# One decoder layer on one core: zeros written in one later transfer, first products and gates reordered, the gates' addition on ScalarE

## The chip, the cores and the metric

The kernel runs on one NeuronCore of a Trainium2 chip. TensorE (PE) multiplies, VectorE (DVE) and GpSimd (POOL) do elementwise work, ScalarE (ACT) does activations, and SyncE (SP) issues most of the transfers. POOL and ACT issue transfers too, each from its own in-order queue. The metric is the time of one execution on the device, in microseconds (us).

## The reference

One causal decoder layer over 512 tokens of width 1024, in float32, batch 1:

```
mod = silu(c) @ w_ada + b_ada            # six vectors: shift, scale, gate, twice
h = rms_norm(x) * (1 + scale1) + shift1
qa, ka, va, qb, kb, vb = split(h @ w_in)
o_dil = dilated_attention(rope(norm(qa)), rope(norm(ka)), va)   # 12 heads in 3 patterns
o_sb = stick_breaking_attention(qb, kb, vb)                     # 4 heads
g_dil, g_sb = split(sigmoid(h @ w_branch_gate))
x = x + gate1 * ((g_dil * (o_dil @ w_branch_dil) + g_sb * (o_sb @ w_branch_sb)) @ w_out)
h2 = rms_norm(x) * (1 + scale2) + shift2
x = x + gate2 * moe(h2)                  # 32 experts in 4 groups, top 2 in the top group
```

Each expert is silu(x @ w_g) * (x @ w_u) @ w_d with weights of 1024x512, 1024x512 and 512x1024: 6.3 MB an expert.

## The kernel before, in words

Each engine has its own program, written out by hand in one order. Engines wait for each other on semaphores (wait_ge), and on each engine everything behind a wait waits too.

**adaLN.** w_ada is read in 24 pieces of 128x2048 (1 MB), eight for each third of the modulation. A piece is multiplied by `ada` (L671 to 676) in four matmuls side by side. The first eight pieces have buffers of their own. The other 16 go through one buffer, `ada_slot`: SP issues a piece only when the semaphore ada_used says that the one before it has been read (L400 to 412). They are used one after each of the projection products 0 to 15. The eighth piece of a third lets DVE add the bias (`mod_round`), and for the first third PE then transposes the result (`mod_columns`), DVE forms the scale and shift columns, and the normalised input is scaled in eight chunks of 128 channels.

**Splitting.** float32 products are made of three passes over a high and a low part, 24 matmuls for a 128x512 output (`split_product`, L717). ACT copies the high part (`split_hi`, L1242; for the input L1257), DVE or POOL subtracts for the low part (`split_lo`, L1503 and L591; for the input L1530).

**Projections.** 24 products (NU) of the input with w_in in six column groups. Product 0 follows the chunks of the input as they come; product 1 comes after it and the adaLN piece behind it. ACT takes each product from PSUM, three banks in turn. For products 8 to 19 DVE and POOL do the norm and the rotary embedding, and PE transposes the result (`transposes_of`).

**Zeros.** The experts' rows are scattered into a DRAM tensor y_rows of 2048x512 that must be zero first. Half of the tile grow is set to zero on POOL (L533), and eight transfers of 512 KB (`clear_rows`, L535 to 539) go out on POOL's queue, two before each of the first four rotary steps. The same half of grow takes a part of the third adaLN third later, so DVE waits for the zeros there (L1498).

**Attention.** Eight steps s of softmax attention. In a step PE does a gate product `gate(s)`, transposes, scores and values; ACT does the exponentials, the gate's exponential (`gate_exp_`, L1306 to 1308) and copies; DVE the masks and maxima (`softmax_max`), the mixing of the patterns (`mix`) and, last in the step, `gate_finish(s)`: one is added (L1694) and the reciprocal taken (L1695). Gate 8 comes after the loop. Then come the four stick-breaking heads. PE: `sb_suffix(h)` (L868), `sb_z(h+1)` (L857), gate 10+2h, a product with the dilated branch (L893), `sb_values(h)` (L877), gate 11+2h. DVE: `sb_copy`, `sb_softplus` (L1734 to 1738), `sb_args` (L1744 to 1747), the gates between them, and `dil_gate`. ACT: `sb_logs` (L1351 to 1354) and `sb_exp`. Gates 10 to 15 share one PSUM bank, so a gate product waits for the exponential of the one before.

**Experts.** SP issues the first expert's weights when the eight branch products are done (br_ps, L449). After that three buffers of 6.3 MB are refilled as they are used. POOL scatters the rows of 30 experts into y_rows, and waits for the zeros before the first.

The tile xn is reused: ada_slot is its words 0 to 2047, the softmax scores of even steps are in 0 to 1023 and of odd steps in 1024 to 2047.

Of the kernel before, what the change touches and what calls it, by code (L numbers as in the profile page):

```python
# [60 lines left out]
def hybrid_layer(nc, x, c, positions, w_ada, b_ada, g_norm_mix, g_norm_ffn, w_in, w_branch_gate,  # L61
# [6 lines left out]
    with ctx:  # L68
# [103 lines left out]
        ada_slot = xnf[:, 0:2048]  # L172
        xg = xnf[:, 2048:3072].rearrange("p (b n) -> p b n", b=2)
# [92 lines left out]
        ada_used = sem("ada_used")  # L266
        mod_rows = sem("mod_rows")
# [237 lines left out]
        def _(pool):  # L505
# [26 lines left out]
            pool.wait_ge(trig_ok, 2)  # L532
            link(pool.memset(grow[64:128, :], 0.0))  # L533

            def clear_rows(i):  # L535

                pool.dma_start(y_rows[4 * SEQ // 8 * i:4 * SEQ // 8 * (i + 1), :].rearrange("(p r) n -> p r n", p=64),
                               grow[64:128, :].unsqueeze(1).to_broadcast([64, 4 * SEQ // 8 // 64, CH])
                               ).then_inc(zero_out, 16)
# [9 lines left out]
            for u in range(QK_FIRST, QK_LAST + 1):  # L549
# [5 lines left out]
                if m < 4:  # L555
                    clear_rows(2 * m)
                    clear_rows(2 * m + 1)
# [19 lines left out]
            pool.wait_ge(ada_used, 3 * KC)  # L577

# [73 lines left out]
            pool.wait_ge(zero_out, 16 * 8)  # L652
# [16 lines left out]
        def _(pe):  # L669
# [25 lines left out]

            pe.wait_ge(crep_ok, 1)
            for k in range(KC):
                pe.wait_ge(ada_in[k], 16)
                ada(k, ada_piece(k), k == 0, k == KC - 1)
            pe.wait_ge(gains_in, 64)  # L700
            pe.transpose(ps[:, 5, 0:KC], gn_rows, ident[0:KC, 0:KC]).then_inc(first_T, 1)
            mod_columns()

# [16 lines left out]
            for u in range(NU):  # L720
                ch, t = divmod(u, NT)
                if u == 0:
                    pe.wait_ge(whi_ok, 1)
                    pe.wait_ge(wlo_ok, 1)
                elif t == 0 or u == 2:
                    pe.wait_ge(whi_ok, 2 * ch + 2)
                    pe.wait_ge(wlo_ok, 2 * ch + 2)
# [4 lines left out]
                for k in range(KC):  # L732
                    if u == 0:
                        pe.wait_ge(hi_ok, k + 1)
                        pe.wait_ge(lo_ok, k + 1)
# [8 lines left out]
                if u < 2 * KC:  # L744
                    if u == 0:
                        pe.wait_ge(mod_rows, 1)
                    if u == KC:
                        pe.wait_ge(mod_rows, 2)
                    pe.wait_ge(ada2_in, 16 * (u + 1))
                    ada(u % KC, ada_slot, u % KC == 0, u % KC == KC - 1)  # L750
# [433 lines left out]
        def _(act):  # L1184
# [121 lines left out]
            def gate_exp_(f):  # L1306
                act.wait_ge(gate_ps, f + 1)
                act.activation(gT[:, f, :], ps[:, gate_bank(f), :], ACT.Exp, scale=-1.0).then_inc(gate_exp, 1)

# [792 lines left out]
```

## Time and profile before

| | before |
|---|---|
| median of 3 runs (lowest to highest) | 975.9 us (972.07 to 976.53) |
| profiled execution: time, span | 974.79 us, 972.7 us |
| busy: PE, DVE, ACT, POOL | 91%, 49%, 20%, 15% of the span |
| chain that ended last | PE 60%, SP's queue 20%, DMA 10%, DVE 6% |
| moved by DMA | 275.04 MB, mean 283 GB/s |
| GB/s in slices of 24.3 us, from 195 to 243 us | 33 and 6 |
| longest idle times of PE before 420 us | 8.00 us to 316.30; 6.23 us to 124.46; 2.73 us to 28.93; 2.67 us to 277.46 and 2.66 us to 40.63 |

The span is the profiled part of the execution; 2.1 us of its time lie around it. The page cuts the span in 40 slices and gives for each the busy share of every engine, the TensorE clock that was granted (1.00 is 2.4 GHz, 0.50 is 1.2 GHz) and the DMA rate. In a timeline a row is a group of like instructions one after another: its start, its length, the engine, the line, the operation, output and input, and in brackets how long the engine had been idle and what ended that. "PEld" is PE's loading of weights and "SPq" the queue of an engine. In the chain each step is followed back to what released it.

### The profile page before, as it was taken

What the parts mean: (1) busy time and instruction counts of PE and PEld (TensorE: products, weight loads), DVE (VectorE), ACT (ScalarE), POOL (GpSimd) and SP (SyncE); (2) the same over time, 40 slices, a digit from 0 to 9 for tenths busy, and PEclk for the clock granted to TensorE, in tenths of its full rate; (3) what the DMA queues carried; (4) which work ended last, traced back from release to release, by engine and by line L of the source; (5) the groups of instructions that cost most, each with busy time, mean ns of one, the idle gap of its engine ahead of it and who ended that gap; (6) DMA issues with size and microseconds to landing.
All of it is one profiled execution on the core that took longest, in us unless ns stands there. A gap on an engine that the chain in (4) does not pass through costs nothing.

```text
span 972.7 us, 11286 instructions
## 1 busy us (share of the span) xinstructions
PE 889.4 (91%) x4193; PEld 513.6 (53%) x4193; DVE 480.5 (49%) x837; ACT 197.5 (20%) x330; POOL 142.0 (15%) x175
## 2 busy tenths in 40 slices
PE   3699889999986999999999999999999998998884
PEld 2266568998865666478654444434443433333331
DVE  2441255627799666643564344433443344243546
ACT  3432123325443233232210000000000000000000
POOL 1000321302341111261200100000000000000110
PEclk9799989999998999999899999999999999999998
DMA  9877876100314020464578999999999999999996
GB/s 345 316 234 253 300 264 220 60 33 6 115 49 142 1 86 1 172 260 173 224 295 355 422 421 421 421 421 420 421 421 421 421 420 423 420 421 423 421 415 247
DMA packets 60189, 275.04 MB, mean 283 GB/s; under 512 B 8868, under 2 KB 21164, under 8 KB 31988
## 3 DMA queue, kind: packets, MB, share of 16 engines
q1 hardware_dynamic: 54772, 264.41, 68.4%
q0 software_dynamic: 4064, 9.19, 2.6%
q10 hardware_dynamic: 1312, 0.87, 0.3%
q8 instruction: 29, 0.48, 0.2%
q14 instruction: 12, 0.10, 0.0%
HBM read 263.71 MB, written 14.70 MB: 286 GB/s over the span
## 4 chain that ended last, share of the span: by engine, by line
PE 60%; SPq 20%; DMA 10%; DVE 6%; issue 3%; ACT 1%; DVEq 0%; POOL 0%; POOLq 0%; ACTq 0%
PE ps L717 23%; SPq L438 15%; PE ps L1078 12%; PE ps L1097 6%; PE ps L1054 4%; DMA arena<-in_w_expert_down 3%; DMA xn<-in_w_ada 3%; SPq L446 3%; PE ps L675 2%; SPq L393 2%; PE ps L901 1%; PE ps L893 1%; DMA arena<-in_w_ada 1%; PE ps L868 1%; PE ps L1064 1%
## 5 line engine op out<-in xcount | busy, mean ns | idle before, releaser
L1078 PE MATMUL ps<-arena,hT 128*64 128x512 f32 x1024 | 228.8, 596 | 5.1 <-DMA arena<-in_w_expert_up 4.4
L1078 PEld LDWEIGHTS ps<-arena,hT 128*64 128x64 f32 x1024 | 70.3, 137 | 146.5 <-issue 132.6
L1097 PE MATMUL ps<-arena,hT 128*64 128x512 f32 x512 | 116.9, 598 | 15.0 <-DMA arena<-in_w_expert_down 14.0
L1955 DVE TENSOR_SCALAR hT<-hT 128x256 f32<-128x256 f32 x32 | 9.4, 293 | 228.5 <-ACT hT L1428 228.5
L717 PE MATMUL ps<-slot_r,xs_r 128*128 128x512 f32 x320 | 107.1, 407 | 0.4 <-issue 0.4
L717 PE MATMUL ps<-xs_r,slot_r 128*128 128x512 f32 x320 | 102.5, 402 | 2.9 <-DVE hT_r L1530 2.9
L717 PE MATMUL ps<-slot_r,hT_r 128*128 128x512 f32 x224 | 88.6, 396 | 0.0
L717 PEld LDWEIGHTS ps<-slot_r,xs_r 128*128 128x128 f32 x320 | 78.0, 264 | 10.8 <-ACT arena L1288 2.5
L1097 PEld LDWEIGHTS ps<-arena,hT 128*64 128x64 f32 x512 | 34.1, 136 | 76.9 <-issue 57.9
L717 PEld LDWEIGHTS ps<-xs_r,slot_r 128*128 128x128 f32 x320 | 59.0, 190 | 19.4 <-issue 6.1
L641 POOL COPY idx<-small 128x1 int32 (+1 forms) x32 | 6.8, 212 | 409.5 <-DVE hT L1977 391.5
L1424 ACT ACTIVATE hT<-ps,slot_rstd 128x512 f32<-128x512 f32 x32 | 22.0, 687 | 203.4 <-PE ps L1054 203.4
L717 PE MATMUL ps<-hT_r,slot_r 128*128 128x512 f32 x160 | 63.0, 394 | 0.0
L1503 DVE TENSOR_TENSOR slot_r<-arena,slot_r 128x2048 fp32r<-128x2048 f32 x14 | 32.0, 2289 | 56.3 <-ACT slot_r L1242 56.3
L591 POOL TENSOR_TENSOR slot_r<-arena,slot_r 128x2048 fp32r<-128x2048 f32 x10 | 46.4, 4650 | 86.8 <-ACT slot_r L1242 86.7
L717 PEld LDWEIGHTS ps<-slot_r,hT_r 128*128 128x128 f32 x224 | 54.5, 243 | 4.6
L1957 DVE RECIPROCAL hT<-hT 128x256 f32<-128x256 f32 x32 | 56.1, 1753 | 1.1
L1428 ACT ACTIVATE hT<-ps 128x256 f32<-128x256 f32 x32 | 12.3, 385 | 215.6 <-PE ps L1078 215.6
L1695 DVE RECIPROCAL arena<-arena 128x512 f32<-128x512 f32 x16 | 53.6, 3353 | 0.5
L1054 PE MATMUL ps<-xs_r,hT_r 128*128 128x512 f32 x128 | 53.8, 421 | 0.0
L1054 PE MATMUL ps<-xn_r,hT_r 128*128 128x512 f32 x128 | 51.2, 400 | 0.0
L1242 ACT ACTIVATE slot_r<-arena 128x2048 fp32r<-128x2048 f32 x24 | 45.5, 1904 | 9.6 <-issue 5.6
(291 smaller groups left out, 1079.2 us busy)
## 6 DMA issues: line engine op xcount, KB each, us to landing
arena<-in_w_expert_gate SPq DMA_DIRECT2D x64, 1024.0 KB, 24.2
arena<-in_w_expert_up SPq DMA_DIRECT2D x64, 1024.0 KB, 26.7
arena<-in_w_expert_down SPq DMA_DIRECT2D x32, 2048.0 KB, 29.4
xn<-in_w_ada SPq DMA_DIRECT2D x16, 1024.0 KB, 5.0
arena<-in_w_in SPq DMA_DIRECT2D x12, 1024.0 KB, 8.3
arena<-in_w_ada SPq DMA_DIRECT2D x8, 1024.0 KB, 14.2
arena<-in_w_branch_gate SPq DMA_DIRECT2D x4, 2048.0 KB, 8.2
xs<-in_x SPq DMA_DIRECT2D x8, 512.0 KB, 8.5
```

The lines of the kernel that those rows point to most:

```text
L438: sp.dma_start(w_gu(b)[:, g, ks].rearrange("p k n -> p (k n)"), src).then_inc(gu_in[b][kh], 16)
L446: sp.dma_start(w_dn(b).rearrange("p (h k) n -> p h (k n)", h=2), src).then_inc(dn_in[b], 16)
L591: pool.tensor_tensor(w_half(w_lo(j), j, half), w_half(w_raw(j), j, half), w_half(w_hi(j), j, half).bitcast(F32), ALU.subtract).then_inc(wl ...
L717: mm = pe.matmul(out_ps, lhsT, rhs, start=(k == 0 and i == 0), stop=(k == KC - 1 and i == 2))
L1054: mm = pe.matmul(ps[:, 6 * half, :], hot_r[:, t, :], part[:, t, half * CH:(half + 1) * CH], start=(t == 0 and part is xs_r), stop=(t == NT ...
L1078: mm = pe.matmul(ps[64 * h:64 * h + 64, 2, :], xeT[:, xb, k, CAP * j:CAP * (j + 1)], w_gu(b)[:, :, k, 256 * h:256 * h + 256], start=(k == ...
L1097: mm = pe.matmul(ps[64 * h:64 * h + 64, 4, :], hhT[:, f % 2, 64 * (f // 2):64 * (f // 2) + 64], w_dn(b)[:, f, h * CH:(h + 1) * CH], start= ...
L1242: act.activation(w_half(w_hi(j), j, half), w_half(w_raw(j), j, half), ACT.Copy).then_inc(whi_ok, 1)
L1424: act.activation(ye if second else xe, ps[:, 6 * half, :], ACT.Copy, scale=slot_rstd[:, 0:1]).then_inc(xe_ok, 1)
L1503: dve.tensor_tensor(w_half(w_lo(j), j, half), w_half(w_raw(j), j, half), w_half(w_hi(j), j, half).bitcast(F32), ALU.subtract).then_inc(wlo ...
L1695: dve.reciprocal(gT[:, f, :], gT[:, f, :]).then_inc(gate_ok, 1)
L1957: dve.reciprocal(hh, hh).then_inc(h_seq, 1)
```

## The change

Four things. The zeros come from a quarter of xn that is free once all adaLN pieces are used, in one transfer after POOL's last rotary step; DVE waits for it before the softmax of step 1, which writes there, and POOL before the first scatter. PE does products 0 and 1 together, chunk by chunk, and the two adaLN pieces after them. Matmuls whose result nobody reads (`idle_work`) are put before the last three of the first eight adaLN pieces and after the transposes of the modulation. ACT adds the one to each gate behind its exponential, and DVE takes only the reciprocal; gate 7 is finished after the last head's output of the mix is stored, and gates 8 to 15 two to a head, after `sb_args`.

```diff
@@ -170,6 +170,7 @@
...
         xnf = xn[:].rearrange("p t n -> p (t n)")
         ada_slot = xnf[:, 0:2048]
+        zeros = xnf[:, 2048 - CH:2048]
         xg = xnf[:, 2048:3072].rearrange("p (b n) -> p b n", b=2)
@@ -264,6 +265,7 @@
...
         crep_ok = sem("crep_ok")
         ada_used = sem("ada_used")
+        gate_one = sem("gate_one")
         mod_rows = sem("mod_rows")
@@ -529,14 +531,6 @@
...
             link(pool.affine_select(negstrict, negstrict, [[1, P]], ALU.is_gt, NEG, base=0, channel_multiplier=-1))
-            pool.wait_ge(trig_ok, 2)
-            link(pool.memset(grow[64:128, :], 0.0))
-
-            def clear_rows(i):
-
-                pool.dma_start(y_rows[4 * SEQ // 8 * i:4 * SEQ // 8 * (i + 1), :].rearrange("(p r) n -> p r n", p=64),
-                               grow[64:128, :].unsqueeze(1).to_broadcast([64, 4 * SEQ // 8 // 64, CH])
-                               ).then_inc(zero_out, 16)
@@ -552,9 +546,6 @@
...
                 if m == KC + 1:
                     columns(1)
-                if m < 4:
-                    clear_rows(2 * m)
-                    clear_rows(2 * m + 1)
                 tt = t + (NT if ch != C_QK0 else 0)
@@ -575,6 +566,9 @@
...
             pool.wait_ge(ada_used, 3 * KC)
+            link(pool.memset(zeros, 0.0))
+            pool.dma_start(y_rows.rearrange("(p r) n -> p r n", p=P),
+                           zeros.unsqueeze(1).to_broadcast([P, 4 * SEQ // P, CH])).then_inc(zero_out, 16)
@@ -649,7 +643,7 @@
...
                 ).then_inc(y_out, 16)
-            pool.wait_ge(zero_out, 16 * 8)
+            pool.wait_ge(zero_out, 16)
             store(0, 0)
@@ -693,13 +687,21 @@
...
                 mm.then_inc(hT_ps, 1)
+            def idle_work(n):
+
+                for _ in range(n):
+                    pe.matmul(ps[:, 4, 0:32 * KC], ident[:], crep[:].rearrange("p k n -> p (k n)"), start=True, stop=True)
+
             pe.wait_ge(crep_ok, 1)
             for k in range(KC):
+                if k >= 5:
+                    idle_work(5 if k == 5 else 3)
                 pe.wait_ge(ada_in[k], 16)
...
             pe.transpose(ps[:, 5, 0:KC], gn_rows, ident[0:KC, 0:KC]).then_inc(first_T, 1)
             mod_columns()
+            idle_work(5)
@@ -717,12 +719,30 @@
...
                 return mm
-            for u in range(NU):
+            def ada_more(u):
+                if u == 0:
+                    pe.wait_ge(mod_rows, 1)
+                if u == KC:
+                    pe.wait_ge(mod_rows, 2)
+                pe.wait_ge(ada2_in, 16 * (u + 1))
+                ada(u % KC, ada_slot, u % KC == 0, u % KC == KC - 1)
+
+            pe.wait_ge(whi_ok, 1)
+            pe.wait_ge(wlo_ok, 1)
+            for k in range(KC):
+                pe.wait_ge(hi_ok, k + 1)
+                pe.wait_ge(lo_ok, k + 1)
+                for u in range(2):
+                    a = [w(0)[:, k, u * P:(u + 1) * P] for w in (w_hi, w_lo)]
+                    mm = split_product(ps[:, u, :], a, [h[:, k, :] for h in (h_hi, h_lo)], k)
+                    if k == KC - 1:
+                        mm.then_inc(proj_done, 1)
+            for u in range(2):
+                ada_more(u)
+
+            for u in range(2, NU):
                 ch, t = divmod(u, NT)
-                if u == 0:
-                    pe.wait_ge(whi_ok, 1)
-                    pe.wait_ge(wlo_ok, 1)
-                elif t == 0 or u == 2:
+                if t == 0 or u == 2:
                     pe.wait_ge(whi_ok, 2 * ch + 2)
@@ -730,9 +750,6 @@
...
                         pe.wait_ge(gain_ok, u - 3 - QK_FIRST + 1)
                 for k in range(KC):
-                    if u == 0:
-                        pe.wait_ge(hi_ok, k + 1)
-                        pe.wait_ge(lo_ok, k + 1)
                     if ch == C_SB:
@@ -742,12 +759,7 @@
...
                 mm.then_inc(proj_done, 1)
                 if u < 2 * KC:
-                    if u == 0:
-                        pe.wait_ge(mod_rows, 1)
-                    if u == KC:
-                        pe.wait_ge(mod_rows, 2)
-                    pe.wait_ge(ada2_in, 16 * (u + 1))
-                    ada(u % KC, ada_slot, u % KC == 0, u % KC == KC - 1)
+                    ada_more(u)
                 if QK_FIRST <= u - 1 <= QK_LAST:
@@ -1306,6 +1318,8 @@
...
                 act.wait_ge(gate_ps, f + 1)
                 act.activation(gT[:, f, :], ps[:, gate_bank(f), :], ACT.Exp, scale=-1.0).then_inc(gate_exp, 1)
+                act.wait_ge(gate_exp, f + 1)
+                act.activation(gT[:, f, :], gT[:, f, :], ACT.Identity, bias=1.0).then_inc(gate_one, 1)
@@ -1495,7 +1509,6 @@
...
                     dve.tensor_copy(grow[0:64, :], modr[0:64, :]).then_inc(gates_kept, 1)
                 if r == 2:
-                    dve.wait_ge(zero_out, 16 * 8)
                     dve.tensor_copy(grow[64:128, :], modr[64:128, :]).then_inc(gates_kept, 1)
@@ -1619,6 +1632,8 @@
...
                     dve.wait_ge(qk_tr, QK_LAST - QK_FIRST + 1)
                     dve.wait_ge(ada_used, 3 * KC)
+                if s == 1:
+                    dve.wait_ge(zero_out, 16)
                 if s >= 2:
@@ -1690,8 +1705,7 @@
...
             def gate_finish(f):
-                dve.wait_ge(gate_exp, f + 1)
-                link(dve.tensor_scalar(gT[:, f, :], gT[:, f, :], 1.0, None, ALU.add))
+                dve.wait_ge(gate_one, f + 1)
                 dve.reciprocal(gT[:, f, :], gT[:, f, :]).then_inc(gate_ok, 1)
@@ -1706,11 +1720,10 @@
...
                 if s - 2 >= NT:
                     out_T(s - 2 - NT)
-                gate_finish(s)
-            gate_finish(8)
+                if s < 2 * NT - 1:
+                    gate_finish(s)
             mix_args(NT - 1)
             mix(NT - 1)
-            out_T(2)
@@ -1753,17 +1766,18 @@
...
             sb_copy(0)
             sb_softplus(0)
-            gate_finish(9)
+            out_T(2)
             out_T(3)
+            gate_finish(2 * NT - 1)
             for h in range(NH):
                 sb_args(h)
+                for f in (8, 9):
+                    gate_finish(2 * h + f)
                 if h < NH - 1:
                     dil_gate(2 * h)
                 if h + 1 < NH:
-                    gate_finish(10 + 2 * h)
                     sb_copy(h + 1)
                     sb_softplus(h + 1)
-                    gate_finish(11 + 2 * h)
                     dil_gate(2 * h + 1)
```

## Rows read from the trace of the kernel before

**Rows 1.** Windows, expert stage: us, busy (count) per engine, PEclk, DMA share, GB/s.

```profile
715.00:930.00 215.00, 199.20 (x917) 77.64 (x916) 85.71 (x170) 15.39 (x29) 18.75 (x29) 1.00 1.01 422
```

**Rows 2.** The chain that ended last: start us, us, what.

```profile
112.23 12.19 DMA xn<-in_w_ada
...
344.11 4.33 PE ps L868 x20
...
898.62 31.55 DMA arena<-in_w_expert_down
```

**Rows 3.** Timeline of PE at the start: start, us, engine, line, op, [idle before].

```profile
34.11 1.94 PE L675 MATMUL ps<-arena,crep 128*32 128x512 f32 x8 [0.76 <-DMA arena<-in_w_ada]
...
36.85 1.12 PE L683 MATMUL ps<-ident,modr 128*128 128x128 f32 x4 [0.61 <-DVE modr L1493]
...
40.63 1.19 PE L717 MATMUL ps<-xs_r,slot_r 128*128 128x512 f32 x2 [2.66 <-DVE hT_r L1530]
...
48.58 1.07 PE L675 MATMUL ps<-xn,crep 128*32 128x512 f32 x8
...
55.25 1.06 PE L675 MATMUL ps<-xn,crep 128*32 128x512 f32 x8
```

**Rows 4.** Timelines of PE and ScalarE's queue, 110 to 142 us.

```profile
111.10 1.07 PE L675 MATMUL ps<-xn,crep 128*32 128x512 f32 x8
...
113.64 5.61 ACTq L1201 DMA_DIRECT2D modr<-in_b_ada  x4
...
124.46 1.93 PE L675 MATMUL ps<-xn,crep 128*32 128x512 f32 x8 [6.23 <-DMA xn<-in_w_ada]
...
133.88 1.06 PE L675 MATMUL ps<-xn,crep 128*32 128x512 f32 x8
...
141.23 1.07 PE L675 MATMUL ps<-xn,crep 128*32 128x512 f32 x8
```

**Rows 5.** Timelines of PE, DVE, ScalarE and POOL, 299 to 343 us.

```profile
299.46 2.42 PE L857 MATMUL ps<-arena 64*128 64x512 f32 x8
...
301.22 3.35 DVE L1695 RECIPROCAL arena<-arena 128x512 f32<-128x512 f32 x1
...
307.71 1.27 ACT L1354 ACTIVATE xn<-xn 128x1280 f32<-128x1280 f32 x1
...
309.65 1.49 DVE L1734 SCALAR_TENSOR_TENSOR xn<-xn 128x1280 f32<-128x1280 f32 x1
...
311.35 9.26 POOL L591 TENSOR_TENSOR slot_r<-arena,slot_r 128x2048 fp32r<-128x2048 f32 x2 [21.50 <-ACT slot_r L1242]
...
311.77 4.48 DVE L1738 TENSOR_TENSOR xn<-xn,strict 128x128 f32<-128x128 f32 x1
...
316.30 2.07 PE L868 MATMUL ps<-xn,tri 128*128 128x512 f32 x2 [8.00 <-DVE xn L1738]
...
324.61 2.42 PE L857 MATMUL ps<-arena 64*128 64x512 f32 x8 [1.55 <-DVE arena L1688]
...
336.66 0.73 PE L717 MATMUL ps<-xs_r,slot_r 128*128 128x512 f32 x2
...
342.44 0.29 DVE L1738 TENSOR_TENSOR xn<-xn,strict 128x128 f32<-128x128 f32 x1
```

**Rows 6.** Two of ScalarE's lines: duration ns min/median/max, first and last start us.

```profile
L1257 ACT ACTIVATE xs_r<-hT x8: 617/630/634, 39.1 to 46.2; 128x512 fp32r<-128x512 f32 x8
...
L1252 ACT ACTIVATE hT<-hT,cols x4: 797/799/801, 39.7 to 45.4; 128x512 f32<-128x512 f32 x4
```

**Rows 7.** Lines 406 and 537: issue durations, and DMA from issue to landing.

```profile
DMA to landing us min/median/max: 4.7/5.0/12.2
...
L537 POOL DMA_DIRECT2D y_rows<-grow x8: 616/628/667, 106.5 to 127.3; - x8
...
DMA to landing us min/median/max: 7.0/9.1/12.9
```

**Rows 8.** Windows of PE, the gap: us, PE busy (count), PEclk, DMA share, GB/s.

```profile
118.30:124.40 6.10, 0.00 (x0) 0.86 1.01 378
```

## The prediction

> **What bounds the kernel now.** I read the page first, then the stages by windows, then the chain that ended last, then the timelines of the stretches that the change touches. TensorE (PE) is busy 91% of the span, but the end is set in the expert stage: from 715 to 930 us the DMA engines are full at 422 GB/s [rows 1], and the chain reaches the last expert's weights through a 31.55 us transfer [rows 2]. What the change touches lies before 406 us. The first expert load is issued when the eight branch products are done, so what is won or lost before that point moves the whole weight stream, and I carry it to the end at one to one. Before that point PE is the bound nearly everywhere; what can be won is where PE stands idle. Three such places matter here: the start of the first product at 40.63, a 6.23 us gap before the adaLN matmuls at 124.46, and the 8.00 us before 316.30 [rows 3 to 5].
>
> **Part 1, the start.** Idle matmuls are added between the last adaLN pieces and after the transposes of the modulation. The 8 matmuls of the last piece took 1.94 us where the same group takes 1.06 later, and the four transposes 1.12 [rows 3]. I take them at the full clock: 0.88 us and, by the same ratio, 0.5 us. So the first product starts 1.3 us earlier, at 39.3. An idle matmul has 256 columns against 512 of an adaLN group of four side by side, so about half a group's 0.9 us (1.06 less the tail of the last): some 0.45. The five, three, three and five of them fit the gaps (2.1 us into the 2.66 before 40.63). If the clock is not up there, the last five take 4.3 us and cost up to 1.6 us: that end goes into the range.
>
> Products 0 and 1 now share the loop over the eight chunks. From the second product's start after 48.58+1.07=49.65 to 55.25, one product takes 5.6 to 5.7 us [rows 3]. ScalarE and DVE made a chunk in about 1 us (eight of ScalarE's copies from 39.1 to 46.2 [rows 6]), so six matmuls a chunk (1.4 us) are no longer starved: both products end at 39.3+2x5.6=50.5. Before, product 1 ended at 55.2 with one adaLN round between. So far a win. But the adaLN slot is a single buffer: the transfer for round 1 is issued only when round 0 has read it. Round 0 now runs 50.5 to 51.6, the transfer takes 5.0 us (the median landing [rows 7]), and nothing is left to put under it, since both products are done. Round 1 starts at 56.7 rather than 55.25, after 5.1 us of idleness. In the gap of 6.1 us before 124.46 the granted clock averaged 0.86, so it had fallen to 1.2 GHz before the gap's end [rows 8], and the group behind took 1.93 us [rows 4]. I take the same here: 0.9 us for round 1 and 1.1 us on the next product (133.88 less 124.46 is 9.42, less 7.35 of a usual round, less 0.9 for the group itself, leaves 1.2). **Sum of part 1: 1.4+0.9+1.1=3.4 us lost.** Bounds: 1.4 lost with the clock kept, 4.7 if the early gain fails too.
>
> **Part 2, the zeros.** Eight transfers of 512 KB that clear y_rows go out between 106.5 and 127.3 from the POOL queue [rows 7]. In that stretch one adaLN transfer took 12.19 us [rows 2] against a median of 5.0 [rows 7]. From 111.10 to 133.88 two rounds took 22.78 us; a usual one is 141.23-133.88=7.35, so 8.1 us were lost: 6.2 of waiting and the rest in the lower clock after it [rows 4]. With the zeros gone from there both go. ScalarE's four bias loads, 5.61 us to issue [rows 4], hold its in-order queue in the same stretch; if they stay that slow, the halves of the next weight split come about 2.2 us late for product 12. So 5.9 to 8.1 us won; I take **8.1**, because the bias loads are small (64 KB each) and the zeros are what was in their way.
>
> The zeros go out as one transfer of 4.2 MB after POOL's last rotary step, at 193. POOL waits for a memset of some 0.6 us, then does three tiny constants, and is next wanted at 235: worth nothing, and the eight issues of 0.62 us taken from between its rotary steps [rows 7] are worth nothing either, as those are not waited for. What is new is DVE's wait before the mask of attention step 1, at 223.6. The transfer has 30 us. At the 422 GB/s of [rows 1] it needs 10 us; if it went at the pace of the small ones, one after another, 8x9.1=73 us. I take it as hidden, since the page shows the DMA engines nearly idle from 195 to 240, and keep the slow end as a rival. The Trainium skill (DMA: Bandwidth & Descriptors, the anatomy of a DMA on the gpsimd path) gives 2.0 us plus bytes over 436 GB/s, an estimate of 11.6 us for this one; no run shows a transfer of that size yet.
>
> **Part 3, the gates.** The addition of one leaves DVE for ScalarE: 0.80 us at most for such a pass over 512 columns [rows 6]. ScalarE has idle time in every attention step, but the pass sits ahead of the copies and of the weight split that follows. In one step (s=5) the split on POOL starts later by it, and a small DVE operation that waits for that split holds the next softmax: I price this at 0.5 us (between 0 and 0.8) lost.
>
> The larger effect is the order on DVE. Gates 7 and 8 (0.4+3.35 us each) stand before the last mix and so before the stick-breaking softplus, which starts at 309.65; without their 7.5 us DVE alone would be ready at about 302 [rows 5]. Head 0's scores are there at 299.46+2.42=301.9, ScalarE's three passes of 1.2 to 1.3 us end at 306.0, and DVE's 2.1 (309.65 to 311.77) and 0.29 give the softplus at 308.4, where it was 316.2 [rows 5]. There its last operation, 0.29 us for the next head, took 4.48, since it began inside POOL's two splits of 9.26 us together [rows 5]. The new softplus is done before that split begins at about 311. PE is free at 308.3, so its suffix products start at 308.5 instead of 316.30 (7.8 us); they run at the full clock, 4.3 us as for head 1 [rows 2], instead of the 6.8 from 316.30 to 323.06 (2.4 us); and the 1.55 us wait before 324.61, for the copy that stood behind gate 9, goes. So gate 10 starts 11.7 us earlier [rows 5].
>
> **Part is given back.** POOL's splits still run from 311.1 to 320.3, and now they meet the mask additions after the suffix. The first begins at 314.5, is held to the end of the first split, the second to the end of the second: the arguments are ready at 320.7. ScalarE then does one exponential, the three passes of head 1 and only then gate 10's exponential, which frees the bank for gate 11: 320.8+1.3+3.9+0.6=326.6. PE reaches that point 11.7 us before 336.66, at 325.0, so it waits 1.7 us and gate 11 starts at 326.7 against 336.66: **9.95 us won** [rows 5]. From there DVE owes two reciprocals (6.7 us) per head, behind the arguments rather than before them; I followed it for heads 1 and 2 and the softplus stays 2 us ahead of PE. At the last head gates 14 and 15 come just before the last two products with the gates, which end about 0.3 us after the merge could start. Sum of part 3: 9.95-0.5-0.3=**9.1 us won** (bounds 6 and 10.5: the lower if the handover at gate 11 or at the last head costs 2 to 3 us more, the upper if only the idle bank wait stays).
>
> The Trainium skill (SBUF — State Buffer, who interferes with whom) says that a DVE operation with two SBUF inputs and a GpSimd operation that reads SBUF lock each other out for a whole instruction. The 4.48 us agree with that. It speaks against this change, since the masks now fall under two splits in a row; if the first addition lost the port to the second split as well, the arguments would come at about 321.3 and part 3 would be 0.6 us smaller.
>
> **Sum.** The profiled execution took 974.8 us: 974.8+3.4-8.1-9.1=961.0. The median shown, 975.9, stands 1.1 above it: 962.
>
> **Rivals.** (A) *The long landing is not the zeros' doing.* Then part 2 is worth nothing: 970. For it: a weight load and the bias loads shared the stretch. Against: 12.19 is also the largest of fifteen landings, and weight loads stood beside others of about 5 [rows 7]. (B) *The gates don't pay:* DVE's deferred reciprocals become the bound over the heads, and PE finds each softplus 2 us late: 4 heads x 2 us, 8 of the 9.1 gone, 970. Against: DVE is 2 us ahead in my count. (C) *The one large zero transfer is slow, the case in which it is slower than before.* Its place is DVE's wait before step 1. It has 30 us; every us beyond that is a us of the whole. At 44 us the gain is used up, at 49 it is 0.5% slower, and at the 73 us of the small ones in a row it is 43-14=29 us slower: 1005. For it: those ran at 7.0 to 12.9 us for 512 KB. Against: they overlapped, eight in under 35 us beside PE's own loads. (D) *The clock survives the new 5 us gap:* part 1 loses only 1.4 and it ends at 960. (E) The change does what it says; the new ordering cannot fail to apply, so no chance is left for that.
>
> **How the numbers follow.** About 0.5% (5 us) is what a measurement can tell from no change, so faster is below 971, slower above 981. My forecast with D, 0.73; A 0.10; B 0.10; C 0.07, of which 0.04 above 981. A and B end at 970, just inside faster, but with the other terms' errors half of each falls above 971: faster 0.73+0.10=0.83, same 0.10+0.03=0.13, slower 0.04. Range: the bounds of the terms added give 4.7-5.9-6=-7 to 1.4-8.1-10.5=-17, that is 959 to 969; the runs shown spread 4 us, so 956 to 970.
>
> **What would show it.** Right: no adaLN landing over 7 us; a new PE gap of about 5 us before round 1 near 51.6 to 56.7, with a low clock behind it; the suffix of head 0 some 12 us earlier (7.8 of its own, 4.7 of parts 1 and 2), with no long idle time before it; a DVE mask addition of 2 to 4 us inside POOL's split; a short PE wait before gate 11; the zeros landing in 10 to 20 us with no DVE wait behind them; the expert stage of the same length to within 2 us. Wrong: a DVE wait on the zeros, a round near 118 still waiting, or PE waiting for softplus at heads 1 to 3.

## The result, and the profile after

| | before | after |
|---|---|---|
| median of 4 runs each (lowest to highest), us | 974.88 (972.07 to 976.53) | 958.40 (957.06 to 960.31) |
| ratio, with its 95% interval | | 0.9835 (0.9805 to 0.9866) |
| profiled execution: time, span, us | 974.79, 972.7 | 957.06, 955.3 |

The median fell by 16.5 us where 13.9 was predicted (975.9 to 962); 958.4 lies in the range of 956 to 970. By the spans of the two profiled executions it is 17.4 us, and that is the difference split up below.

The page of the kernel after: span, busy shares, the granted clock and the DMA rate in 40 slices, and the chain's shares by engine.

```profile
span 955.3 us, 11342 instructions
...
PE 889.4 (93%) x4225; PEld 516.5 (54%) x4225; DVE 475.2 (50%) x821; ACT 206.8 (22%) x346; POOL 138.2 (14%) x168
...
PEclk9989999999999999999999999999999999999998
...
GB/s 344 330 232 221 273 214 185 88 177 7 117 48 146 89 1 114 136 236 131 352 299 399 424 421 421 420 421 421 420 421 422 421 422 421 421 422 424 421 416 220
...
PE 65%; SPq 14%; DMA 12%; DVE 4%; issue 2%; ACT 2%; DVEq 0%; POOL 0%; POOLq 0%; ACTq 0%
```

The weight stream at 421 GB/s is the same; it began earlier. To see where the time went, the start of the same piece of work is read in both traces (rounds count from 0; round 8 is the ninth, which an expectation may call round 9):

| start of, us | before | after | difference | won or lost since the line above |
|---|---|---|---|---|
| first product | 40.63 | 40.37 | -0.3 | -0.3 |
| adaLN round 8 | 104.4 | 107.1 | +2.7 | +3.0: the joint products |
| adaLN round 15 | 163.27 | 157.85 | -5.4 | -8.1: the zeros |
| first scores | 214.5 | 209.1 | -5.4 | 0 |
| transposes of step 6 | 277.46 | 272.23 | -5.2 | +0.2: ScalarE's additions |
| suffix of head 0 | 316.30 | 302.86 | -13.4 | -8.2: the gates |
| gate 11 | 336.66 | 320.48 | -16.2 | -2.7 |
| first output product | 417.34 | 401.19 | -16.2 | 0 |
| end of the span | 972.7 | 955.3 | -17.4 | -1.3 |

**The start.** PE's timeline of the kernel after (start, length, engine, line, operation; idle time before it and what ended it). L669 is an adaLN group, L677 the transposes, L693 the idle matmuls, L719 the products.

```profile
35.18 1.06 PE L669 MATMUL ps<-arena,crep 128*32 128x512 f32 x8 [0.84 <-DMA arena<-in_w_ada]
...
37.06 0.66 PE L677 MATMUL ps<-ident,modr 128*128 128x128 f32 x4 [0.66 <-DVE modr L1507]
37.55 2.32 PE L693 MATMUL ps<-crep,ident 128*128 128x256 f32 x10
40.37 0.70 PE L719 MATMUL ps<-xs_r,slot_r 128*128 128x512 f32 x2 [0.50 <-DVE hT_r L1543]
...
51.47 1.06 PE L669 MATMUL ps<-xn,crep 128*32 128x512 f32 x8
57.25 1.93 PE L669 MATMUL ps<-xn,crep 128*32 128x512 f32 x8 [4.72 <-DMA xn<-in_w_ada]
```

Against [rows 3] the adaLN group and the transposes ran at the full clock, and the two products flowed into each other. Then PE stood 4.72 us for the single adaLN buffer: the chain names that transfer, issued as round 0 ended. Behind it the clock was low, as the windows of PE show (stretch, length, PE busy with its count, granted clock, DMA share, GB/s); a value between 0.50 and 1.00 is a mean over a stretch that had both levels.

```profile
51.40:57.25 5.85, 1.13 (x9) 0.90 0.63 220
59.10:66.60 7.50, 7.50 (x32) 0.74 1.02 331
```

**The zeros.** First PE where the 6.23 us wait of [rows 4] was, then the landings of the adaLN pieces (L408), then the zeros' transfer (L570) on POOL.

```profile
113.79 1.06 PE L669 MATMUL ps<-xn,crep 128*32 128x512 f32 x8
...
121.40 1.07 PE L669 MATMUL ps<-xn,crep 128*32 128x512 f32 x8 [0.48 <-DMA xn<-in_w_ada]
...
128.46 1.06 PE L669 MATMUL ps<-xn,crep 128*32 128x512 f32 x8
```

```profile
DMA to landing us min/median/max: 4.5/4.7/6.4
```

```profile
L570 POOL DMA_DIRECT2D y_rows<-xn x1: 1172/1172/1172, 188.6 to 188.6; - x1
...
DMA to landing us min/median/max: 14.7/14.7/14.7
```

No adaLN piece took more than 6.4 us, where one took 12.2 [rows 7]. The zeros land at about 203 (188.6 and 14.7 us), ahead even of the first scores at 209.1, so DVE's new wait before the softmax of step 1 costs nothing.

**The gates.** Timelines of all engines from the softplus of head 0 to gate 11. L1751 and L1760 are DVE's masks before and after the suffix, L880 the suffix, L869 the next head's scores, L585 POOL's splits, L1320 and L1322 ScalarE's exponential and addition of a gate, L1709 the reciprocal.

```profile
302.51 0.29 DVE L1751 TENSOR_TENSOR xn<-xn,strict 128x128 f32<-128x128 f32 x1
...
302.84 0.63 ACT L1322 ACTIVATE arena<-arena 128x512 f32<-128x512 f32 x1
302.86 1.12 PE L880 MATMUL ps<-xn,tri 128*128 128x512 f32 x2 [0.46 <-DVE xn L1751]
...
305.36 9.40 POOL L585 TENSOR_TENSOR slot_r<-arena,slot_r 128x2048 fp32r<-128x2048 f32 x2 [20.73 <-ACT slot_r L1254]
...
307.39 2.42 PE L869 MATMUL ps<-arena 64*128 64x512 f32 x8
...
309.74 0.73 PE L719 MATMUL ps<-xs_r,slot_r 128*128 128x512 f32 x2
...
310.33 4.58 DVE L1760 TENSOR_TENSOR xn<-xn,small 128x128 f32<-128x128 f32 x1
...
314.83 6.55 DVE L1709 RECIPROCAL arena<-arena 128x512 f32<-128x512 f32 x2
314.94 1.27 ACT L1372 ACTIVATE xn<-xn 128x1280 f32<-128x1280 f32 x1 [7.87 <-DVE xn L1760]
...
320.48 0.73 PE L719 MATMUL ps<-xs_r,slot_r 128*128 128x512 f32 x2 [0.99 <-ACT arena L1320]
```

PE's 8.00 us before the suffix [rows 5] are 0.46. The operation held by POOL is now the last mask after the suffix (4.58 us), and what is late behind it is gate 11, by 0.99 us. The chain runs through that mask.

### The profile page after: what moved, and what is told of

Its sections match the earlier page's. It is cut to its first block, busy times and chain, and to the rows that moved or that the text cites. A ratio compares the mean times of both kernels' runs of the same rounds, so it can differ in the third digit from the quotient of the medians.

```text
span 955.3 us, 11342 instructions
## 1 busy us (share of the span) xinstructions
PE 889.4 (93%) x4225; PEld 516.5 (54%) x4225; DVE 475.2 (50%) x821; ACT 206.8 (22%) x346; POOL 138.2 (14%) x168
## 4 chain that ended last, share of the span: by engine, by line
PE 65%; SPq 14%; DMA 12%; DVE 4%; issue 2%; ACT 2%; DVEq 0%; POOL 0%; POOLq 0%; ACTq 0%
PE ps L719 25%; PE ps L1090 14%; SPq L440 11%; PE ps L1109 7%; DMA arena<-in_w_expert_down 6%; PE ps L1066 4%; PE ps L669 2%; PE ps L880 2%; SPq L395 2%; DMA xn<-in_w_ada 2%; DMA arena<-in_w_ada 2%; SPq L448 1%; PE ps L913 1%; PE ps L905 1%; PE ps L834 1%
## 5 line engine op out<-in xcount | busy, mean ns | idle before, releaser
L719 PE MATMUL ps<-slot_r,xs_r 128*128 128x512 f32 x320 | 106.2, 404 | 0.4 <-issue 0.4
L719 PE MATMUL ps<-xs_r,slot_r 128*128 128x512 f32 x320 | 102.2, 401 | 1.5 <-ACT arena L1320 1.0
L719 PE MATMUL ps<-slot_r,hT_r 128*128 128x512 f32 x224 | 88.1, 393 | 0.0
L719 PEld LDWEIGHTS ps<-slot_r,xs_r 128*128 128x128 f32 x320 | 77.3, 262 | 10.5 <-ACT arena L1300 2.5
L719 PEld LDWEIGHTS ps<-xs_r,slot_r 128*128 128x128 f32 x320 | 59.5, 191 | 17.5 <-issue 2.9
L719 PE MATMUL ps<-hT_r,slot_r 128*128 128x512 f32 x160 | 63.1, 394 | 0.0
L585 POOL TENSOR_TENSOR slot_r<-arena,slot_r 128x2048 fp32r<-128x2048 f32 x10 | 46.3, 4645 | 76.8 <-ACT slot_r L1254 76.7
L719 PEld LDWEIGHTS ps<-slot_r,hT_r 128*128 128x128 f32 x224 | 54.2, 242 | 4.5
L1709 DVE RECIPROCAL arena<-arena 128x512 f32<-128x512 f32 x16 | 53.0, 3331 | 0.0
```

What stands on the lines that cost most here:

```text
L585: pool.tensor_tensor(w_half(w_lo(j), j, half), w_half(w_raw(j), j, half), w_half(w_hi(j), j, half).bitcast(F32), ALU.subtract).then_inc(wl ...
L719: mm = pe.matmul(out_ps, lhsT, rhs, start=(k == 0 and i == 0), stop=(k == KC - 1 and i == 2))
L1709: dve.reciprocal(gT[:, f, :], gT[:, f, :]).then_inc(gate_ok, 1)
```

## The experiments

Each kernel stands beside runs of the kernel before on the same chip (medians 973.7 to 974.9), with four executions of its own, `b_gates` with six, `b_front` and `a_no_idle` with ten. The ratio with its interval is a measured value of its own and not the quotient of the medians. Where the text compares a variant with the kernel after (958.4), the two medians come from different chips, and those of before differ by up to 1.2 us: a difference of 2 us or less is weak by itself, and the stretches of the traces carry the argument. Of each kernel there is one trace. "Step 6" is the stretch from the transposes of step 6 to those of step 7, 11.40 us at the full clock: it turned out to decide 3 us, which is told under `a_mid_p9`.

| kernel | median (lowest to highest), us | ratio, interval | span | scores to first output product |
|---|---|---|---|---|
| `b_zeros` | 962.5 (962.1 to 963.3) | 0.9895 (0.9853 to 0.9936) | 961.5 | 204.3 |
| `b_gates` | 965.1 (962.6 to 967.9) | 0.9912 (0.9883 to 0.9941) | 965.9 | 195.1 |
| `b_front` | 978.5 (975.1 to 981.7) | 1.0040 (1.0011 to 1.0069) | 979.4 | 202.8 |
| `a_no_idle` | 960.3 (958.3 to 966.2) | 0.9882 (0.9853 to 0.9910) | 957.9 | 192.1 |
| `a_apart` | 954.9 (953.2 to 958.5) | 0.9820 (0.9767 to 0.9873) | 956.7 | 195.1 |
| `a_ada_first` | 953.6 (951.2 to 956.4) | 0.9796 (0.9751 to 0.9841) | 954.6 | 194.7 |
| `a_ada_mid` | 951.5 (949.2 to 952.3) | 0.9787 (0.9733 to 0.9841) | 949.5 | 192.1 |
| `a_pool9` | 957.6 (955.3 to 959.3) | 0.9850 (0.9795 to 0.9905) | 956.1 | 191.0 |
| `a_old_order` | 960.5 (960.4 to 961.6) | 0.9895 (0.9811 to 0.9979) | 958.8 | 195.2 |
| `a_add_dve` | 957.9 (956.1 to 961.6) | 0.9859 (0.9773 to 0.9944) | 959.8 | 193.8 |
| `a_mid_p9` | 953.1 (952.4 to 953.8) | 0.9818 (0.9734 to 0.9901) | 950.6 | 194.1 |
| `a_all` | 951.6 (951.4 to 952.9) | 0.9804 (0.9721 to 0.9888) | 949.7 | 192.3 |

Before has 202.8 in the last column, after 192.1.

**`b_zeros`: the kernel before, with the zeros' part alone.**

```diff
-                if m < 4:
-                    clear_rows(2 * m)
-                    clear_rows(2 * m + 1)
...
+            link(pool.memset(zeros, 0.0))
+            pool.dma_start(y_rows.rearrange("(p r) n -> p r n", p=P),
+                           zeros.unsqueeze(1).to_broadcast([P, 4 * SEQ // P, CH])).then_inc(zero_out, 16)
```

> The kernel before with the one large zero transfer alone. Theory (the small zeros slow the adaLN transfer and with it the clock): 8.1 us less, the round at 124 waits no more than 1.1 us, and the 4.2 MB land within 15 to 20 us, 8 us or more ahead of their first user. Rival A (the long landing comes from the weight and bias loads of that stretch): the wait near 118 stays above 4 us and the time is within 2 us of before.

Measured: 12.4 us under before's median; by the interval of the ratio 6 to 14, which holds the 8.1 expected. From round 9 (108.57) to round 15 it took 152.1-108.6=43.5 us against 163.3-111.1=52.2: 8.7 won there. The long landing was the zeros' doing, and the one large transfer is hidden. In the two traces another 2.5 us was there by round 8, ahead of anything the edit touches: this execution missed before's two waits of 1.12 and 1.04 us for adaLN pieces, and its first product started at 39.73 rather than 40.63.

**`b_gates`: the kernel before, with ScalarE's addition and the new order of the gates.**

```diff
+                act.activation(gT[:, f, :], gT[:, f, :], ACT.Identity, bias=1.0).then_inc(gate_one, 1)
...
-                    gate_finish(10 + 2 * h)
...
-                    gate_finish(11 + 2 * h)
...
+                for f in (8, 9):
+                    gate_finish(2 * h + f)
```

> The kernel before with both gate edits alone (the addition on ScalarE and the new order on DVE). Theory: 9.1 to 10.7 us less, the suffix of head 0 7.5 to 8 us earlier, DVE's mask addition still held 4 to 5 us by POOL's split. Rival B (DVE's reciprocals become the bound over the heads): at most 2 us less.

Measured: 9.8 us under before's median. The wait for the zeros stayed (6.66 us at 123.55). From the scores to the output product 195.1 us instead of 202.8, and 3 of those 195.1 are a low clock in step 6 that before and after did not have; without it 192.0, the same as after.

**`b_front`: the kernel before, with the idle matmuls and the joint products.**

```diff
+            for k in range(KC):
...
+                for u in range(2):
+                    a = [w(0)[:, k, u * P:(u + 1) * P] for w in (w_hi, w_lo)]
+                    mm = split_product(ps[:, u, :], a, [h[:, k, :] for h in (h_hi, h_lo)], k)
```

> The kernel before with the idle matmuls and the joint first products alone. Theory (single adaLN buffer leaves nothing under the second transfer): 2.5 to 4.5 us more, with an idle gap of PE near 5 us before the second late adaLN piece. Rival (the joint loop pays for itself through the clock and the fuller chunks): 1 to 3 us less.

Measured: 3.7 us slower than before by the medians, interval of the ratio wholly above 1 (1 to 7 us). Two rows of PE's timeline:

```profile
58.29 1.94 PE L675 MATMUL ps<-xn,crep 128*32 128x512 f32 x8 [5.14 <-DMA xn<-in_w_ada]
...
130.17 1.94 PE L675 MATMUL ps<-xn,crep 128*32 128x512 f32 x8 [8.67 <-DMA xn<-in_w_ada]
```

The new wait is there. With the zeros still in eight pieces the second wait grew to 8.67 us, so what the start costs is not quite independent of part 2.

**`a_no_idle`: the kernel after, without the idle matmuls.**

```diff
-                if k >= 5:
-                    idle_work(5 if k == 5 else 3)
...
-            idle_work(5)
```

> The changed kernel without the idle matmuls. If they keep the clock up at the start and that reaches the products: the pieces near 31 and 35 us and the transposes take 1.9 and 1.1 us again, the joint products run their first microseconds at 1.2 GHz, and 2 to 3 us are lost. If they are idle in both senses (the pieces are set by their transfers, the products by the chunks): within 1 us of 958.4.

Rows of PE's timeline:

```profile
33.96 1.93 PE L669 MATMUL ps<-arena,crep 128*32 128x512 f32 x8 [0.82 <-DMA arena<-in_w_ada]
...
36.70 1.12 PE L677 MATMUL ps<-ident,modr 128*128 128x128 f32 x4 [0.61 <-DVE modr L1499]
...
54.37 1.07 PE L669 MATMUL ps<-xn,crep 128*32 128x512 f32 x8
```

The low clock is back, and it lasts into the products: from the first one to round 0 took 13.9 us (40.47 to 54.37) against 11.1. The output product came 4.0 us later than after's; of that the medians show 1.9, and the ranges overlap. So what the idle matmuls are worth lies behind the start of the first product (0.1 us later here), not before it.

The other traces bear on this. In the ten kernels with idle matmuls the last three adaLN groups took 1.06 or 1.07 us. Of the four without, three had the low clock in the last two (1.93 or 1.94 us), but `b_zeros` did not:

```profile
34.09 1.07 PE L668 MATMUL ps<-arena,crep 128*32 128x512 f32 x8 [1.67 <-DMA arena<-in_w_ada]
...
35.97 1.12 PE L676 MATMUL ps<-ident,modr 128*128 128x128 f32 x4 [0.66 <-DVE modr L1486]
```

Its transposes and first product matmuls (1.19 us) were at the low clock all the same, as in the other three. Nor do the idle matmuls always hold the clock: in `a_apart`, and likewise in `b_front`, it fell at the transposes. The last idle matmuls took 3.88 us (3.71 in `b_front`) instead of 2.32, and the first product started at 40.70 (40.88), later than in any of the four kernels without them (39.73 to 40.66).

```profile
37.17 3.88 PE L693 MATMUL ps<-crep,ident 128*128 128x256 f32 x10
```

**`a_apart`: the kernel after, products 0 and 1 apart again, the idle matmuls kept.**

```diff
-            for u in range(2):
-                ada_more(u)
-
-            for u in range(2, NU):
+            for u in range(NU):
```

> The changed kernel with products 0 and 1 apart again, one adaLN piece behind each as before; the idle matmuls stay. If the joint loop is what the front loses by: round 1 (the second late piece) starts near 54 us instead of 57.2, without a gap of 4.7 us before it, product 2 starts 4 us earlier and the time is 954 to 955 us. If the front's loss came from the idle matmuls: no change from 958.4.

Measured: 3.5 us under after by the medians. Round 1 at 54.6 instead of 57.25, no wait before it, round 8 at 101.86 instead of 107.12: the joint products, joined in this way, cost 5.3 us by round 8. 1.7 of it was given back at round 10 (a 1.74 us wait for its piece), and 3 in step 6 to the low clock.

**`a_ada_first`: the kernel after, round 0 ahead of the joint products, round 1 behind them (and three idle matmuls there instead of five).**

```diff
-            idle_work(5)
+            idle_work(3)
...
+            ada_more(0)
             pe.wait_ge(whi_ok, 1)
...
-            for u in range(2):
-                ada_more(u)
+            ada_more(1)
```

> The changed kernel with the first late adaLN piece used before the joint products instead of behind them (and three idle matmuls rather than five after the transposes), so that the transfer of the next piece runs under both products. If the single buffer is what the front loses by: the gap of 4.7 us at 52.5 goes and product 2 starts 6 to 7 us earlier; of that 5 to 7 us reach the end, for 952 us. If the later rounds are bound by the transfers anyway: product 2 starts earlier but waits for adaLN pieces give most of it back, 957 us.

Measured: 4.8 us under after. The second wait is gone, but PE waited 2.05 us at 40.72 for piece 0, which is issued at 23.15 beside the other loads and took 17.4 us.

**`a_ada_mid`: the same, round 0 after the third chunk of the joint products.**

```diff
                     if k == KC - 1:
                         mm.then_inc(proj_done, 1)
-            for u in range(2):
-                ada_more(u)
+                if k == 2:
+                    ada_more(0)
+            ada_more(1)
```

> The changed kernel with the first late adaLN piece used after the third chunk of the joint products. In a_ada_first that piece was not there until 40.7 us, so PE waited 2.05 us for it. Here nothing should wait: round 1 starts near 52.5 us, 2 us earlier than in a_ada_first, for 951.5 to 952.5 us. If the later transfers take it back: 953.5.

PE's adaLN groups of this kernel:

```profile
44.80 1.06 PE L669 MATMUL ps<-xn,crep 128*32 128x512 f32 x8
...
52.83 1.07 PE L669 MATMUL ps<-xn,crep 128*32 128x512 f32 x8
```

Measured: 951.5, the fastest of all: 6.9 us under after by the medians, 22 under before. Neither group has an idle time before it, since the piece for round 1 comes in under the last five chunks. Round 8 starts at 99.50 (107.12 in after), and the output product 7.6 us before after's.

**`a_pool9`: the kernel after; POOL waits for the arguments before its second split under head 0.**

```diff
+                    if (j, half) == (9, 1):
+                        pool.wait_ge(arg_ok, 1)
                     split_lo(j, half)
```

> The changed kernel with a wait on POOL: its second split of weight piece 9 starts only when DVE's arguments of head 0 are done. If the 4.6 us mask addition is held by that split and this is what makes PE wait before gate 11: the addition takes 0.3 us, the arguments are ready 4.2 us earlier, the wait of 0.98 us before gate 11 goes, and 1 us is won in all, as the rest was hidden behind PE. If the addition is slow for another reason: it stays above 4 us.

POOL's and DVE's timelines:

```profile
306.31 4.53 POOL L585 TENSOR_TENSOR slot_r<-arena,slot_r 128x2048 fp32r<-128x2048 f32 x1 [20.74 <-ACT slot_r L1256]
311.67 4.62 POOL L585 TENSOR_TENSOR slot_r<-arena,slot_r 128x2048 fp32r<-128x2048 f32 x1 [0.83 <-DVE xn L1762]
```

```profile
311.29 0.29 DVE L1762 TENSOR_TENSOR xn<-xn,small 128x128 f32<-128x128 f32 x1
```

The mask took 0.29 us instead of 4.58, so the 4.58 are waiting for POOL's split (below, the lock) and no work of its own. PE's wait before gate 11 went, and suffix to output product took 97.25 us against 98.33: 1.1 us. The whole lock was worth no more; the medians, 0.8 apart, can't tell it.

**`a_old_order`: the kernel after, with before's order of the gates on DVE; the addition stays on ScalarE.**

```diff
-                for f in (8, 9):
-                    gate_finish(2 * h + f)
...
+                    gate_finish(10 + 2 * h)
...
+                    gate_finish(11 + 2 * h)
```

> The changed kernel with DVE's gates in the order of before; the addition stays on ScalarE. If the order is what won: head 0's suffix waits again near 6 to 7 us (the two reciprocals, 6.7 us, ahead of the softplus; the 0.8 us of their additions are gone), and 6 to 9 us are lost, for 965 to 967 us. If taking the addition off DVE was enough, since then DVE meets POOL's split less: 2 us lost at most.

DVE's, POOL's and PE's timelines:

```profile
303.59 0.29 DVE L1752 TENSOR_TENSOR xn<-xn,strict 128x128 f32<-128x128 f32 x1
```

```profile
303.83 8.99 POOL L585 TENSOR_TENSOR slot_r<-arena,slot_r 128x2048 fp32r<-128x2048 f32 x2 [20.79 <-ACT slot_r L1254]
```

```profile
303.93 2.07 PE L880 MATMUL ps<-xn,tri 128*128 128x512 f32 x2 [3.10 <-DVE xn L1752]
```

Measured: 2.1 us over after by the medians, 3.1 from the scores to the output product. That is between what the two theories expected. Undoing the order brought back a wait of 3.10 us and the low clock behind it, not 8.00. With two additions fewer on DVE (0.42 and 0.37 us in before) the last mask of the softplus begins 0.24 us before POOL's split does, and takes 0.29 us where it took 4.48 [rows 5]: together 5.0 us, and the two waits differ by 4.9.

**`a_add_dve`: the kernel after, with the addition back on DVE.**

```diff
-                dve.wait_ge(gate_one, f + 1)
+                dve.wait_ge(gate_exp, f + 1)
+                link(dve.tensor_scalar(gT[:, f, :], gT[:, f, :], 1.0, None, ALU.add))
```

> The changed kernel with the addition of one back on DVE, in the new order. If the order is what won: 0.4 us for each gate is hidden in DVE's 2 us of slack, within 1.5 us of 958.4. If the move to ScalarE carries a real share: 2 to 4 us lost, by additions of gates 8 and 9 held by POOL's split or a softplus that comes too late for PE.

Measured: 957.9 against after's 958.4, with runs that overlap: no difference. Scores to output product 193.8, of which 2.7 are the low clock in step 6: 191.1 without it. Before's 202.8, the order alone 191.1, the addition alone 195.2 (each with parts 1 and 2 in place), both 192.1: the order does all of it, and the addition, which would do most of it alone, adds nothing beside the order.

**`a_mid_p9`: `a_ada_mid` and `a_pool9` together.**

```diff
+                if k == 2:
+                    ada_more(0)
...
+                    if (j, half) == (9, 1):
+                        pool.wait_ge(arg_ok, 1)
```

> The changed kernel with both edits that paid: the first late adaLN piece after the third chunk, and POOL's second split of piece 9 behind the arguments of head 0. The two places are apart, so the gains add: 951.5 less 0.9, 950.6 us.

Measured: 953.1, 1.5 us over `a_ada_mid` where 0.9 under was expected: the gains did not add. It keeps the 1.1 us after the suffix (299.12 to 396.38 is 97.26) but lost 3.0 in step 6. The first transposes of step 6 in PE's timeline, then the same stretch by windows, columns as above: each time after, then `a_ada_mid`, then this kernel.

```profile
272.23 1.09 PE L815 MATMUL ps<-ident,xn 128*128 128x128 f32 x8 [2.93 <-ACT xn L1328]
```

```profile
264.69 1.09 PE L816 MATMUL ps<-ident,xn 128*128 128x128 f32 x8 [2.92 <-ACT xn L1329]
```

```profile
265.54 1.09 PE L818 MATMUL ps<-ident,xn 128*128 128x128 f32 x8 [2.94 <-ACT xn L1331]
```

```profile
272.23:283.63 11.40, 9.79 (x58) 1.00 0.06 15
```

```profile
264.69:276.09 11.40, 9.79 (x59) 1.00 0.09 18
```

```profile
265.54:279.96 14.42, 14.42 (x58) 0.64 0.07 19
```

All three come out of the same idle time, 2.92 to 2.94 us before the transposes of step 6, with the same work behind it. In two the clock stayed at 2.4 GHz, in one it fell to 1.2 GHz for most of the stretch: 3.0 us.

**`a_all`: `a_mid_p9`, and POOL waits for DVE's first mix (o_ok) before its first split of weight 8.**

```diff
                 if i in (1, 2):
+                    if i == 1:
+                        pool.wait_ge(o_ok, 1)
                     split_lo(8, i - 1)
```

> a_mid_p9 with one more wait on POOL: its first split of weight piece 8 starts only after DVE has mixed token tile 0. If the 2.9 us that PE waits before the transposes of step 6 come from that split holding a small DVE operation: this wait falls below 1 us and 1 to 3 us are won, 948 to 949.5. If the split only meets the next DVE operations instead (or comes late for gate 8): no gain or up to 2 us lost.

DVE's and POOL's timelines, then PE's:

```profile
266.72 4.61 POOL L585 TENSOR_TENSOR slot_r<-arena,slot_r 128x2048 fp32r<-128x2048 f32 x1
```

```profile
267.77 3.60 DVE L1651 TENSOR_SCALAR stats<-stats 128x4 f32<-128x4 f32 x1
```

```profile
274.51 1.69 PE L820 MATMUL ps<-ident,xn 128*128 128x128 f32 x8 [2.83 <-ACT xn L1333]
```

Measured: 951.6, the same as `a_ada_mid`. The wait before step 6 went, and one of 2.83 us came before step 7, with the low clock: the second of the two splits now meets the four-column maximum of the next step.

## Why the prediction was right, and where its sizes were off

**Part 1, predicted 3.4 lost; 2.7 by the two traces, 4.5 and 5.2 against `b_gates` and `b_zeros`, 3.7 by the medians of `b_front` (its longer wait for the zeros included).** The mechanism was right: both products end together (51.5; predicted 50.5), nothing lies under the transfer (4.72 us; 5.1), the clock falls. Three terms were off. The early gain was 0.3 us rather than 1.3: the clock was up as forecast, but the last piece came 1.1 us later than in before (35.18 against 34.11 [rows 3]). That is no chance: its group starts at 34.68 to 35.31 in the ten kernels with idle matmuls and at 33.96 to 34.15 in the four without, `a_apart` (idle matmuls, no joint products) among the first and `a_no_idle` among the second. The piece is issued at the same time (20.62 in after, 20.52 in before) and takes 14.52 us instead of 13.55. So the idle matmuls put off the last piece, a cost that the prediction did not have; why they do stays open. Round 1 and the product behind it cost 2.7 us over the usual 6.65 (57.25 to 66.57 is 9.32), not 2.0. Against that, before's own execution waited 1.12 and 1.04 us for pieces at rounds 3 and 7, which was in its time and not in my sum; `b_zeros` and `b_gates`, with the same start, reached round 8 at 101.9 and 102.6 where it did at 104.4. Against them the loss is 4.5 and 5.2, near or beyond the bound of 4.7. That 2.7 came out near 3.4 is partly luck: my terms for the start were too favourable, and before's own waits hid it. Rival D, the clock surviving, fell.

**Part 2, predicted 8.1; 8.1, and 8.7 alone.** The wait and the low clock behind it went, and rival A fell with `b_zeros`. The zeros took 14.7 us (13.5 in `b_zeros`); I had said 10 to 20. 4.2 MB in that time are 285 GB/s. The estimate from the Trainium skill (DMA: Bandwidth & Descriptors, the anatomy of a DMA on the gpsimd path) was 11.6 us, so the trace does not quite agree, and the trace decides; with 30 us of room either is hidden. Rival C fell.

**Part 3, predicted 9.1; 10.7.** Step by step, from the first scores: the suffix came 8.0 us earlier of its own (7.8 less 0.5 for ScalarE's pass at s=5). That pass is 0.63 us long, and 0.2 us of it reached PE: the term of 0.5 was too large. From the suffix to gate 10 took 6.9 us (302.86 to 309.74) where before took 10.7 (316.30 to 326.96): 3.8 won, 3.95 predicted. The give-back was 0.99 us at gate 11 rather than 1.7; 0.3 to 0.4 of that is that POOL's splits began 0.3 us earlier than I had put them, and the arguments with them. The 0.3 us at the last head did not show. The lock on the masks is real, and `a_pool9` prices it at 1.1 us. Here the Trainium skill (SBUF — State Buffer, who interferes with whom) and the trace agree: a mask of 0.29 us took 4.58 under the split. Rival B fell: no wait for a softplus at heads 1 to 3.

What the text did not foresee is how the two edits of part 3 share their gain. I had the order down as the larger effect and the addition as a small cost, and by `a_add_dve` that is right. But by `a_old_order` the addition alone would have won 7.6 of it, by letting one mask begin 0.24 us ahead of a split; the prediction had the split's place right and did not ask what else would move the mask out of it.

**The end.** From the output product on the two kernels took 555.4 and 554.1 us, within the 552.8 to 556.6 of all runs, so the shift was carried one to one, as assumed.

By the spans the forecast was 3.6 us short (13.8 against 17.4): 0.7 in part 1, nothing in part 2, 1.6 in part 3, and 1.3 in the last stage, which lies in its spread.

## What to carry to other kernels

When two pieces of work are joined to keep an engine fed, look at what used to run between them: a single-buffered transfer that was hidden by the second now stands bare, and putting its reader inside the joint loop (`a_ada_mid`) won 6.9 us over the kernel after, where undoing the joining won 3.5. Small transfers from another queue that nobody waits for can still be what a waited-for transfer is late by; move them to where the DMA engines are idle. Two edits that relieve the same wait don't add up, so try each alone before either is credited.

## What the runs showed of the hardware that I had not expected

- The clock after a wait of 2.65 to 2.94 us is not settled by the length of the wait. Of the kernels with such a wait before step 6, after, before, `b_front`, `a_no_idle`, `a_ada_mid`, `a_pool9` and `a_old_order` kept 1.00 for the stretch behind it (11.40 us); `b_zeros` had 0.73 (12.83 us), and `b_gates`, `a_ada_first`, `a_apart`, `a_add_dve` and `a_mid_p9` had 0.64 to 0.66 (14.1 to 14.5 us). What decides it stays open. It moved these profiled executions by up to 3 us, more than several of the edits, and must be taken out before stages are compared. With one trace per kernel it isn't shown whether it goes by the kernel or by the execution; the mean granted clock over a whole execution was 0.985, 0.986, 0.988 and 0.992 in the four of after, of which the profiled one had the highest, 0.991 to 0.994 in `a_ada_mid` and 0.986 to 0.989 in `a_mid_p9`.
- A DVE operation on 128x4 elements took 3.52 to 3.81 us inside a POOL split, where the same line takes 0.17 in other steps. Making POOL wait for one such operation moved the lock to the next (`a_all`).
- The start is not the same from one execution to the next: with that code untouched, round 8 began at 101.9, 102.6 and 104.4.
